# Two transformer blocks and a mixture of experts on one core: GpSimd's subtractions in four pieces, and loop end, latent norm and attention loads in another order

## The chip, the core and the metric

The kernel runs on one core of one Trainium2 chip. A core has TensorE (PE in the rows; PEld is its weight load), VectorE (DVE), ScalarE (ACT), GpSimd (POOL) and a queue for transfers, SyncE (SP). Each engine works through its own list of instructions in the order in which it is written, and waits on semaphores (counters) where it needs another engine's result. The metric is the time of one execution on the device, in microseconds (us); less is better.

## The reference

Two networks run one after the other on 256 tokens of 1024 features, all in float32.

```python
for i in range(2):                       # first network
    sh1, sc1, g1, sh2, sc2, g2 = ada(c, ada_w[i], ada_b[i])     # 6 x 1024 from a 1024 x 6144 matrix
    h_l = rmsnorm(x, norm1_g[i]) * (1 + sc1) + sh1
    if i == 0:   # latent attention over 256 + 256 tokens, beside a short convolution, then w_o
        out_l, _ = even_mixer(h_l, h_c, w_in, ..., w_o)
    else:        # Fourier transform over tokens and features, then w_fourier
        out_l = fourier_mixer(h_l, w_fourier)
    x = x + g1 * out_l
    x = x + g2 * swiglu(rmsnorm(x, norm2_g[i]) * (1 + sc2) + sh2, w1[i], w3[i], w2[i])   # 1024 -> 2816 -> 1024
# second network: window attention and a linear recurrence, then 32 experts, 4 for each token
x = x + gt1 * parallel_mixer(h, ...)
x = x + gt2 * moe_ffn(h, w_router, w_gu, w_down, ...)
return rms_norm(x, g_final)
```

In the latent attention the projection `h @ w_in` has 384 query latents (`cq`), 256 key and value latents (`ckv`) and 32 position features (`k_pe`). The latents are normed, then multiplied by `w_uq` and `w_ukv`.

## The kernel before

Everything lies with features on the 128 partitions and tokens in columns. One launch goes through these stages: the first modulation columns; 18 *blocks* of `w_in`; latent norm, queries and keys; attention in 16 tiles (8 heads by 2 halves of the tokens); 8 blocks of `w_o`; the gated layer of 22 feature slices; the Fourier mixer with 8 blocks; the second gated layer; the second network's mixer; the experts. All of it is written out by hand: the order of instructions on an engine is the order of the code.

**Blocks.** Block `b` is 1024 by 128 weights (512 KB). SP loads it into `raw` (`blk`), once the block three before has been split (`s_hi`, `s_lo`). ScalarE rounds it to the high part `wh` (`block_hi`, L1289), GpSimd subtracts and gets the low part `wl` (`block_lo`, L1711; 34 blocks), and TensorE multiplies in 24 matmuls: high by high, high by low, low by high (`block_product`, L673 to L675). The product of block `b` goes to PSUM bank `b % 2`, so block `b` may start only when VectorE has fetched block `b - 2` (`evacuate`, L1855, which counts `s_ev`). Blocks 10 to 13 (`B_CC`) and 14 to 17 (`B_CU`) belong to the convolution. Blocks 26 to 33 (`B_F`) are those of the Fourier mixer.

**Latent norm.** After block 9 TensorE sums the squares of `cq` and `ckv`, ScalarE takes the roots, and VectorE forms the reciprocals and scales. For `ckv` that stands behind the evacuation of block 10 (`B_CC`): the reciprocal of 512 columns (L1922), two scalings (L1924), one product of `k_pe` (L1926).

**Updates ("ada").** The modulation of later stages is a product of a 1024 by 6144 matrix with one vector. VectorE does it in the gaps: update `n` multiplies a loaded strip of 128x1024 (`araw`, 512 KB) and adds it to `acc` (L1761, or L1760 for the first of eight). `araw` has two buffers: the load of strip `n` is issued when update `n - 2` is done. Every eight updates TensorE turns the sum into columns (`ada_columns`, L609), and the first update of the next eight waits for that. One update stands in each of the first 13 tiles of the attention loop.

**Attention.** For tile `i` TensorE forms scores (L803), VectorE takes the row's maximum (L2008), ScalarE the exponentials (L1401), VectorE the reciprocal of the sum (L2020), ScalarE scales (L1413), TensorE turns the tile (L810) and multiplies by the values (L820).

**Gated layers.** `ffn(l)` runs slices 2 to 21 in loops of four. Its result stands in PSUM, and VectorE adds it to `x` (L2090) after the last product has been counted in `s_fdn`. Then TensorE sums the loop's updates (`loop_rows`, L637), and after ScalarE's squares of `x` (L1299) it forms the norm's sums (`norm_sums`, L654).

## Time and profile before

| What | Value |
|---|---|
| Median of 3 runs | 1834.28 us (1832.84 to 1837.6) |
| The profiled execution | 1836.75 us, its span 1834.5 us |
| TensorE's mean granted clock | 0.958 of full |
| TensorE busy | 1687.9 us (92%) |
| VectorE busy | 778.8 us (42%) |
| ScalarE busy | 421.1 us (23%) |
| GpSimd busy | 103.3 us (6%), 34 subtractions in 92.2 us |
| Read from memory | 584.26 MB, 319 GB/s over the span |

The profiled execution's time is 2.25 us more than its span, and 2.47 us more than the median. Times in the rows count from the start of the span. A row of the timeline gives start, duration, engine, line, operation, what is written and read, how many instructions are merged into the row, and in brackets how long the engine had been idle before it and whose end released it. A row of a table of windows gives each engine's busy time in that stretch, then TensorE's granted clock (1.00 is 2.4 GHz, 0.50 is 1.2 GHz), the share of the transfer engines and their rate.

### The profile page before, as it was taken

The numbers are of one execution on the slowest core, as the hardware profiler recorded it, in microseconds if no ns is written. First come the engines' busy times: TensorE is split into PE (matmuls) and PEld (weight loads), VectorE is DVE, ScalarE is ACT, GpSimd is POOL, SyncE is SP. The second block draws the span as 40 slices with busy tenths as digits, with TensorE's granted clock in tenths as the row PEclk, the third lists the DMA queues.
The fourth block names the chain that finished last, engine by engine and source line by source line (L and its number), as shares of the span: only waits on it lengthen the run. The fifth ranks groups of instructions, "written<-read, shape, count | busy, mean of one in ns | idle before, by whom it ended". The sixth has DMA issues, their size and how long they took to land.

```text
span 1834.5 us, 23890 instructions
## 1 busy us (share of the span) xinstructions
PE 1687.9 (92%) x9312; PEld 1064.2 (58%) x9312; DVE 778.8 (42%) x1230; ACT 421.1 (23%) x669; POOL 103.3 (6%) x53
## 2 busy tenths in 40 slices
PE   6889899999899999999999999999978998799876
PEld 2873489999589999778443434344423443344222
DVE  5757668887548887554221122222201111122012
ACT  2324544443334443363100000000000000000001
POOL 1623010000310000020000000000000000000000
PEclk8898899999999999999999999999988999899988
DMA  8722648887528888615799999999999999999995
GB/s 309 274 81 95 198 133 284 300 309 260 204 81 287 306 310 300 268 68 219 316 407 421 421 421 421 421 421 422 421 421 421 420 422 420 421 414 421 421 421 210
DMA packets 100427, 586.57 MB, mean 320 GB/s; under 512 B 12048, under 2 KB 13328, under 8 KB 44976
## 3 DMA queue, kind: packets, MB, share of 16 engines
q1 hardware_dynamic: 100336, 585.35, 81.4%
q8 instruction: 58, 0.95, 0.2%
q14 instruction: 33, 0.27, 0.0%
HBM read 584.26 MB, written 1.05 MB: 319 GB/s over the span
## 4 chain that ended last, share of the span: by engine, by line
PE 78%; DMA 10%; DVE 6%; SPq 3%; ACT 1%; issue 1%; POOL 0%; DVEq 0%; ACTq 0%
PE psum L1160 23%; PE psum L1176 11%; PE psum L855 4%; PE psum L857 4%; PE psum L856 4%; SPq L418 3%; PE psum L1136 3%; DMA mraw<-gu_dram 3%; PE psum L1189 2%; PE psum L946 2%; PE psum L870 2%; PE psum L869 2%; PE psum L868 2%; DMA araw<-ada_dram 2%; PE psum L1042 2%; PE psum L673 2%
## 5 line engine op out<-in xcount | busy, mean ns | idle before, releaser
L1160 PE MATMUL psum<-mraw,xsat 128*64 128x512 f32 (+2 forms) x1640 | 412.4, 648 | 54.2 <-DMA mraw<-gu_dram 39.6
L1160 PEld LDWEIGHTS psum<-mraw,xsat 128*64 128x64 f32 (+2 forms) x1640 | 136.0, 144 | 305.4 <-issue 304.3
L1176 PE MATMUL psum<-mraw,xsat 128*64 128x512 f32 (+2 forms) x856 | 204.7, 614 | 17.4 <-DMA mraw<-dn_dram 10.2
L855 PE MATMUL psum<-ah,wh 128*128 128x256 f32 x704 | 200.6, 285 | 3.9 <-DVE al L1820 3.6
L856 PE MATMUL psum<-al,wh 128*128 128x256 f32 x704 | 199.2, 283 | 0.0
L857 PE MATMUL psum<-ah,wl 128*128 128x256 f32 x704 | 199.2, 283 | 0.0
L1176 PEld LDWEIGHTS psum<-mraw,xsat 128*64 128x64 f32 (+2 forms) x856 | 68.0, 139 | 133.0 <-issue 130.9
L855 PEld LDWEIGHTS psum<-ah,wh 128*128 128x128 f32 x704 | 135.1, 192 | 6.7 <-DVE al L1820 3.6
L856 PEld LDWEIGHTS psum<-al,wh 128*128 128x128 f32 x704 | 135.1, 192 | 0.0
L857 PEld LDWEIGHTS psum<-ah,wl 128*128 128x128 f32 x704 | 135.1, 192 | 0.0
L2332 DVE TENSOR_TENSOR oacc<-psum,oacc 128x512 f32<-128x512 f32 x60 | 38.7, 686 | 219.9 <-PE psum L1189 219.9
L1160 PE MATMUL psum<-mlast,xsat 128*64 128x512 f32 (+2 forms) x408 | 119.7, 640 | 0.0
L1711 POOL TENSOR_TENSOR wl<-raw,wh 128x1024 fp32r<-128x1024 f32 x34 | 92.2, 2732 | 437.6 <-ACT wh L1289 425.9
L1677 ACT ACTIVATE xsat<-psum 128x512 f32<-128x512 f32 x16 | 9.6, 597 | 432.0 <-PE psum L1209 432.0
L1876 DVE TENSOR_TENSOR wl<-raw,wh 128x1024 fp32r<-128x1024 f32 x88 | 103.7, 1220 | 0.0
L868 PE MATMUL psum<-mh,wh 128*128 128x256 f32 x352 | 99.6, 283 | 0.0
L869 PE MATMUL psum<-ml,wh 128*128 128x256 f32 x352 | 99.6, 283 | 0.0
L870 PE MATMUL psum<-mh,wl 128*128 128x256 f32 x352 | 99.6, 283 | 0.0
L673 PE MATMUL psum<-ah,wh 128*128 128x256 f32 (+1 forms) x272 | 84.0, 309 | 13.8 <-DVE kbuf L1855 6.2
L2344 DVE COPY ymo<-psum 128x512 f32<-128x512 f32 x15 | 10.4, 691 | 196.0 <-PE psum L1176 196.0
L1431 ACT ACTIVATE wh<-raw 128x2048 fp32r<-128x2048 f32 x44 | 83.9, 1907 | 27.4 <-PE psum L675 24.8
L674 PE MATMUL psum<-al,wh 128*128 128x256 f32 (+1 forms) x272 | 82.5, 303 | 0.0
(362 smaller groups left out, 2423.6 us busy)
## 6 DMA issues: line engine op xcount, KB each, us to landing
mraw<-gu_dram SPq DMA_DIRECT2D x205, 1024.0 KB, 19.0
mraw<-dn_dram SPq DMA_DIRECT2D x107, 1024.0 KB, 25.6
araw<-ada_dram SPq DMA_DIRECT2D x128, 512.0 KB, 4.7
mlast<-gu_dram SPq DMA_DIRECT2D x51, 1024.0 KB, 19.7
raw<-ffa_dram SPq DMA_DIRECT2D x44, 1024.0 KB, 7.6
raw<-ffb_dram SPq DMA_DIRECT2D x44, 512.0 KB, 5.7
mlast<-dn_dram SPq DMA_DIRECT2D x21, 1024.0 KB, 23.9
raw<-blk_dram SPq DMA_DIRECT2D x34, 512.0 KB, 4.6
```

Of the source, the lines that this page charges most:

```text
L673: mm(o, wh[:, w], ah3[:, j, 0:width], start=(j == 0), stop=False)
L855: mm(o, wh[:, w0:w0 + P], ah3[:, j, 0:T], start=(j == 0), stop=False)
L856: mm(o, wh[:, w0:w0 + P], al3[:, j, 0:T], start=False, stop=False)
L857: last = mm(o, wl[:, w0:w0 + P], ah3[:, j, 0:T], start=False, stop=(j == DJ - 1))
L868: mm(o, wh[:, w0:w0 + P], a, start=first and j % 2 == 0, stop=False, skip_group_check=True)
L869: mm(o, wh[:, w0:w0 + P], b_, start=False, stop=False, skip_group_check=True)
L870: last = mm(o, wl[:, w0:w0 + P], a, start=False, stop=end, skip_group_check=True)
L1160: last = mm(ps[4 + n][a * w:(a + 1) * w, :], xs[:, k * P + a * w:k * P + (a + 1) * w], slots[slot][:, i * 2 * D + n * 512:i * 2 * D + (n + ...
L1176: last = mm(ps[n][a * w:(a + 1) * w, :], at[:, k * P + a * w:k * P + (a + 1) * w], slots[slot][:, i * D + n * 512:i * D + (n + 1) * 512], ...
L1431: A(wh[:, w], raw[:, w], ACT.Copy).then_inc(s_fhi, 1)
L1711: sub = lambda o, a, b: nc.gpsimd.tensor_tensor(o, a, b.bitcast(F32), ALU.subtract)
L1876: ins = TTn(wl[:, w], raw[:, w], f32(wh[:, w]), ALU.subtract)
```

## The change

It has five parts.

1. `block_lo` does its subtraction in four instructions of 256 columns, not in one of 1024. The semaphore is counted by the last.
2. The norm of `ckv` is spread out: the reciprocal in two halves, and the scalings behind the evacuations of later blocks. TensorE's product that needs the result moves from after block 14 to after block 16.
3. Loads of strips 28 to 34 go between the loads of blocks 24 and 25 and of the first gated slices. Tile 5 of the attention has no update; tile 13 has one.
4. At the end of a gated layer VectorE adds the result to `x` as soon as each pair of feature tiles is finished (a new semaphore, `s_fend`), and two more updates move behind that. ScalarE's rounding of blocks 26 to 28 moves behind the next norm's root, with GpSimd's subtraction of them; blocks 29 to 31 are rounded between copies of the Fourier product.
5. Behind the next norm stand four updates, not two. One semaphore is shared by two uses, so that `s_fend` finds room.

VectorE at the latent norm, blocks 10 to 14 (`rstd` is the reciprocal, `xc` holds `ckv`, `kbuf` the evacuated blocks), before:

```order
L1855 COPY kbuf<-psum 128x256
L1922 RECIPROCAL rstd<-rt 128x512
L1924 SCALAR_TENSOR_TENSOR xc<-xc,vec,rstd 128x512 x2
L1926 TENSOR_SCALAR psq<-kpe,vec 32x512
L1855 COPY kbuf<-psum 128x256 x3
L1911 TENSOR_TENSOR kbuf<-psum,kbuf 128x256 x4
```

and now:

```order
L1866 COPY kbuf<-psum 128x256
L1933 RECIPROCAL rstd<-rt 128x256
L1866 COPY kbuf<-psum 128x256
L1935 RECIPROCAL rstd<-rt 128x256
L1866 COPY kbuf<-psum 128x256
L1938 SCALAR_TENSOR_TENSOR xc<-xc,vec,rstd 128x512
L1866 COPY kbuf<-psum 128x256
L1938 SCALAR_TENSOR_TENSOR xc<-xc,vec,rstd 128x512
L1922 TENSOR_TENSOR kbuf<-psum,kbuf 128x256
L1940 TENSOR_SCALAR psq<-kpe,vec 32x512
```

Each of the three evacuations of blocks 11 to 13 now has at most one longer operation ahead of it.

ScalarE at the end of the first gated layer (`sg`, `mh` are the last slice's; `warm` loads the table for roots; `wh` are the blocks 26 to 31), before:

```order
L1452 ACTIVATE sg<-psum 128x256
L1456 ACTIVATE mh<-mm_ 128x256
L1289 ACTIVATE wh<-raw 128x1024 x3
L1293 ACT_TABLE_LOAD
L1293 ACTIVATE warm<-vec 1x1
L1299 ACTIVATE work<-x 128x256 x8
L1303 ACTIVATE lrow<-psum 128x1024
L1307 ACTIVATE rt<-psum,vec 128x256
L1289 ACTIVATE wh<-raw 128x1024 x3
L1500 ACTIVATE vdft<-psum 128x512 x8
```

and now:

```order
L1465 ACTIVATE sg<-psum 128x256
L1469 ACTIVATE mh<-mm_ 128x256
L1306 ACT_TABLE_LOAD
L1306 ACTIVATE warm<-vec 1x1
L1312 ACTIVATE work<-x 128x256 x8
L1316 ACTIVATE lrow<-psum 128x1024
L1320 ACTIVATE rt<-psum,vec 128x256
L1302 ACTIVATE wh<-raw 128x1024 x3
L1507 ACTIVATE vdft<-psum 128x512 x8
L1510 ACTIVATE ah<-psum 128x256 x2
L1302 ACTIVATE wh<-raw 128x1024
```

The three roundings that stood between the last slice and the squares of `x` stand behind the root.

VectorE at the end of the second gated layer, from the last slice's low part to the mixer's first evacuations (`acc<-araw` are updates 138 to 143, `lam` and `nsink` the second network's small constants), before:

```order
L2053 TENSOR_TENSOR ml<-mm_,mh 128x256
L1761 SCALAR_TENSOR_TENSOR acc<-araw,vec,acc 128x1024 x2
L2090 SCALAR_TENSOR_TENSOR x<-psum,mod,x 128x256 x8
L1761 SCALAR_TENSOR_TENSOR acc<-araw,vec,acc 128x1024 x2
L2114 SCALAR_TENSOR_TENSOR lam<-vec 128x4
L2115 TENSOR_SCALAR hbias<-vec 128x8
L2117 RECIPROCAL rstd<-rt 128x256
L1788 TENSOR_TENSOR mod<-psum,vec 128x40
L1802 SCALAR_TENSOR_TENSOR gs<-mod,vec 128x8
L2121 TENSOR_TENSOR work<-x,rstd 128x256 x8
L1761 SCALAR_TENSOR_TENSOR acc<-araw,vec,acc 128x1024 x2
L2124 TENSOR_SCALAR nsink<-vec 128x8
```

and now:

```order
L2067 TENSOR_TENSOR ml<-mm_,mh 128x256
L2105 SCALAR_TENSOR_TENSOR x<-psum,mod,x 128x256 x8
L1772 SCALAR_TENSOR_TENSOR acc<-araw,vec,acc 128x1024 x2
L2129 SCALAR_TENSOR_TENSOR lam<-vec 128x4
L2130 TENSOR_SCALAR hbias<-vec 128x8
L2132 RECIPROCAL rstd<-rt 128x256
L1799 TENSOR_TENSOR mod<-psum,vec 128x40
L1813 SCALAR_TENSOR_TENSOR gs<-mod,vec 128x8
L2136 TENSOR_TENSOR work<-x,rstd 128x256 x8
L1772 SCALAR_TENSOR_TENSOR acc<-araw,vec,acc 128x1024 x4
L2139 TENSOR_SCALAR nsink<-vec 128x8
```

Two updates moved from ahead of the additions to `x` to behind them, and two from ahead of the reciprocal to behind the norm's products. The diff of the rest:

```diff
@@ SP @@
-            for b in range(B_O + NRAW, B_F):
+            for b in range(B_O + NRAW, B_F - 2):
                 blk(b)
+            ada(28)
+            ada(29)
+            blk(B_F - 2)
+            ada(30)
+            blk(B_F - 1)
+            ada(31)
+            ada(32)
...
                 ffn_a(l, 0, ffna_d[l, 0])
+                if l == 0:
+                    ada(33)
                 ffn_b(l, 0, ffnb_d[l, 0])
                 if l == 0:
+                    ada(34)
                     sp.wait_ge(s_lo, B_O + NRAW)
                 ffn_a(l, 1, ffna_d[l, 1])
@@ PE @@
-                if b == B_CU:
+                if b == B_CU + 2:
                     pe.wait_ge(s_par, MLA_IN)
...
+                        if end and j in (1, 3, 5):
+                            last.then_inc(s_fend, 1)
                     last.then_inc(s_fdn, 1)
@@ POOL @@
             def block_lo(b):
                 pool.wait_ge(s_hi, b + 1)
-                s = slice(SPLIT[b] * D, (SPLIT[b] + 1) * D)
-                sub(wl[:, s], raw[:, RAW[b]:RAW[b] + D], wh[:, s]).then_inc(s_lo, 1)
-
-            for b in range(B_F + NRAW):
+                for q in range(0, D, PIECE):
+                    w0, r0 = SPLIT[b] * D + q, RAW[b] + q
+                    last = sub(wl[:, w0:w0 + PIECE], raw[:, r0:r0 + PIECE], wh[:, w0:w0 + PIECE])
+                last.then_inc(s_lo, 1)
+
+            for b in range(B_F):
                 block_lo(b)
             pool.wait_ge(s_h, 3 * DJ)
-            for b in range(B_F + NRAW, B_2):
+            for b in range(B_F, B_2):
                 block_lo(b)
@@ DVE @@
-                if i < 13:
-                    ada(27 + i)
+                if i < 5 or 6 <= i < 14:
+                    ada(27 + i if i < 5 else 26 + i)
...
-                for j in range(2, 4):
-                    ada(base_n + 40 + j)
-                dve.wait_ge(s_fdn, 1 + (l + 1) * NF)
                 for j in range(DJ):
+                    if j == 6:
+                        dve.wait_ge(s_fdn, 1 + (l + 1) * NF)
+                    elif j % 2 == 0:
+                        dve.wait_ge(s_fend, 3 * l + j // 2 + 1)
                     STT(x[:, j, :], ps[4 + j // 2][:, (j % 2) * T:(j % 2 + 1) * T], m_col(g_gate, j), x[:, j, :],
                         ALU.mult, ALU.add).then_inc(s_x, 1)
-                for j in range(4, 6):
+                for j in range(2, 4):
                     ada(base_n + 40 + j)
```

## Rows read from the trace of the kernel before

**Rows 1.** Table of windows: the experts' stretch; columns as told above
```profile
886.70:1812.00 925.30, 850.25 (x3880) 351.91 (x3876) 176.37 (x324) 50.96 (x81) 0.00 (x0) 0.96 1.01 418
```
**Rows 2.** Whom TensorE waited for before 886 us: total, times, longest
```profile
PE psum L810 <- ACT psq L1413: 10.2, 7, 5.1
...
PE psum L673 <- DVE xc L1855: 4.1, 1, 4.1
```
**Rows 3.** Timeline of VectorE at the latent norm, and TensorE's block 13 behind it
```profile
98.89 3.34 DVE L1922 RECIPROCAL rstd<-rt 128x512 f32<-128x512 f32 x1
102.27 5.13 DVE L1924 SCALAR_TENSOR_TENSOR xc<-xc,vec,rstd 128x512 f32<-128x512 f32 x2
107.44 2.45 DVE L1926 TENSOR_SCALAR psq<-kpe,vec 32x512 f32<-32x512 f32 x1
...
110.49 0.55 PE L673 MATMUL psum<-ah,wh 128*128 128x256 f32 x1 [6.22 <-DVE kbuf L1855]
```
**Rows 4.** Table of windows: TensorE's clock in three stretches at the lower level, one at the upper
```profile
109.24:116.00 6.76, 5.51 (x26) 5.54 (x27) 1.42 (x4) 0.00 (x0) 2.87 (x2) 0.50 0.71 227
...
191.20:198.00 6.80, 4.46 (x12) 2.58 (x13) 5.72 (x12) 4.04 (x8) 0.00 (x0) 0.50 0.57 157
...
215.00:232.00 17.00, 15.32 (x64) 7.78 (x63) 11.51 (x26) 12.44 (x26) 0.00 (x0) 1.00 0.58 174
471.10:477.80 6.70, 3.30 (x8) 2.68 (x9) 0.05 (x1) 6.36 (x13) 4.65 (x2) 0.50 0.98 349
```
**Rows 5.** Timeline of VectorE in the attention: updates 28 and 32
```profile
190.52 1.28 DVE L1761 SCALAR_TENSOR_TENSOR acc<-araw,csil,acc 128x1024 f32<-128x1024 f32 x1 [5.52 <-DMA araw<-ada_dram]
...
206.91 0.75 DVE L1760 TENSOR_SCALAR acc<-araw,csil 128x1024 f32<-128x1024 f32 x1 [5.32 <-PE psum L609]
```
**Rows 6.** Timeline of TensorE: turns of tiles 1, 9 and 11, updates' columns
```profile
186.30 1.06 PE L810 MATMUL psum<-con,psq 128*128 128x128 f32 x4
...
204.86 1.95 PE L609 MATMUL psum<-con,acc 128*128 128x1 f32 x16
...
218.85 0.65 PE L810 MATMUL psum<-con,psq 128*128 128x128 f32 x4 [0.56 <-ACT psq L1413]
...
224.30 0.66 PE L810 MATMUL psum<-con,psq 128*128 128x128 f32 x4 [0.56 <-ACT psq L1413]
```
**Rows 7.** Timeline: one strip's load with the queue empty, and its update
```profile
244.24 0.33 SPq L398 DMA_DIRECT2D araw<-ada_dram  x1
...
248.12 1.28 DVE L1761 SCALAR_TENSOR_TENSOR acc<-araw,csil,acc 128x1024 f32<-128x1024 f32 x1 [1.29 <-DMA araw<-ada_dram]
```
**Rows 8.** Timeline after the gated layers: ScalarE, TensorE (first layer), TensorE (second)
```profile
470.62 2.00 ACT L1289 ACTIVATE wh<-raw 128x1024 fp32r<-128x1024 f32 x2 [9.23 <-DMA raw<-blk_dram]
...
474.50 5.38 PE L654 MATMUL psum<-work,con 128*128 128x256 f32 x16 [6.54 <-ACT work L1299]
...
742.09 3.72 PE L654 MATMUL psum<-work,con 128*128 128x256 f32 x16
```
**Rows 9.** Timeline of VectorE, then TensorE, after the second gated layer
```profile
749.59 2.77 DVE L2121 TENSOR_TENSOR work<-x,rstd 128x256 f32<-128x256 f32 x8
752.28 2.68 DVE L1761 SCALAR_TENSOR_TENSOR acc<-araw,vec,acc 128x1024 f32<-128x1024 f32 x2
...
758.00 0.76 DVE L1855 COPY q<-psum 128x256 f32<-128x256 f32 x2
...
758.57 3.69 PE L946 MATMUL psum<-work,raw 128*128 128x256 f32 x16 [0.27 <-DVE q L1855]
```
**Rows 10.** GpSimd's and VectorE's operations: at the first norm, the context norm, later
```profile
34.00 7.34 POOL L1711 TENSOR_TENSOR wl<-raw,wh 128x1024 fp32r<-128x1024 f32 x3 [33.55 <-ACT wh L1289]
...
54.09 2.58 DVE L1869 TENSOR_TENSOR al<-work,ah 128x256 fp32r<-128x256 f32 x1
...
806.46 0.61 POOL L1735 TENSOR_TENSOR acc<-xg 128x256 f32<-128x256 f32 x1 [57.80 <-ACT xg L1534]
...
818.08 1.32 POOL L1735 TENSOR_TENSOR acc<-xg 128x256 f32<-128x256 f32 x1 [1.20 <-ACT xg L1534]
```

More of the change, by code:

```diff
@@ L47 @@
 NRAW = 3
+PIECE = 256
 SPLIT = [b % 6 for b in range(B_O)] + [0, 1, 4, 5, 2, 3, 4, 5] * 2
@@ L348, in build @@
         s_lg, s_tk, s_tke, s_mask, s_cum, s_route, s_ht, s_htok, s_flag = [sem(n) for n in (
-            "logits", "top_values", "top_exp", "chosen", "slot_counts", "routed", "h_turned", "h_tokens", "overflow_known")]
+            "logits", "top_values", "top_exp", "chosen", "slot_counts", "routed", "tokens_and_output_turned", "h_tokens", "overflow_known")]
         s_order, s_pick, s_gpp, s_gpc = [sem(n) for n in ("experts_ranked", "ranks_set", "places_product", "places_copied")]
@@ L359, in build @@
         s_last = sem("last_output_copied")
-        s_ot, s_fy = sem("out_turned"), sem("final_chunk")
+        s_fy, s_fend = sem("final_chunk"), sem("ffn_last_tiles")
         def sq_cols(n):
@@ L530, in _ @@
             ffn_first(0)
-            for n in range(28, 48):
+            for n in range(35, 48):
                 ada(n)
@@ L1271, in _ @@
                 mm(out_tile(j), ymo[:, j * P:(j + 1) * P], stt[:, (NU - 1) % 3, :], start=False, stop=True,
-                   skip_group_check=True).then_inc(s_ot, 1)
+                   skip_group_check=True).then_inc(s_ht, 1)
             norm_sums(6)
@@ L1477, in ffn @@
                         down_hi(NF - 1, (NF - 1) % 2, 16 * ((NF - 1) // 2 + 1))
-                if l == 0:
-                    act.wait_ge(s_fgu, NF - 1)
-                    block_hi(B_F)
-                    block_hi(B_F + 1)
-                    act.wait_ge(s_fdn, NF)
-                    block_hi(B_F + 2)
             norm_squares(1, x_by_blocks(B_O))
@@ L1495, in _ @@
             act.wait_ge(s_fdn, 1 + NF)
-            for b in range(B_F + NRAW, B_2 - 2):
+            for b in range(B_F, B_F + NRAW):
                 block_hi(b)
@@ L1503, in _ @@
                 A(ah3[:, c, 0:T], ps[c % 2][:, 0:T], ACT.Copy).then_inc(s_f2h, 1)
+                if c in (1, 3, 5):
+                    block_hi(B_F + NRAW + c // 2)
             last_blocks(1, B_2)
@@ L1921, in _ @@
                     dve.wait_ge(s_cqn, 3)
-                    link(V_.reciprocal(rstd[:, :], rt[:, :]))
-                    for j in range(2):
-                        STT(ckv[:, j, :], ckv[:, j, :], V("kvg", j), rstd[:, :], ALU.mult, ALU.mult).then_inc(s_cqn, 1)
+                    link(V_.reciprocal(rstd[:, 0:T], rt[:, 0:T]))
+                if b == B_CC + 1:
+                    link(V_.reciprocal(rstd[:, T:2 * T], rt[:, T:2 * T]))
+                if b in (B_CC + 2, B_CC + 3):
+                    j = b - B_CC - 2
+                    STT(ckv[:, j, :], ckv[:, j, :], V("kvg", j), rstd[:, :], ALU.mult, ALU.mult).then_inc(s_cqn, 1)
+                if b == B_CU:
                     TS(pbuf[NOPE:QD, 0, :], kpe[NOPE:QD, :], vec[NOPE:QD, _V["kgain"]:_V["kgain"] + 1], None, ALU.mult
@@ L2097, in _ @@
             norm(2, _V["n1"] + 8, 6)
-            ada(94)
-            ada(95)
+            for n in range(92, 96):
+                ada(n)
             for c in range(8):
@@ L2121, in _ @@
                 TTn(work[:, j, 0:T], x[:, j, :], rstd[:, 0:T], ALU.mult).then_inc(s_nt, 1)
-            ada(142)
-            ada(143)
+            for n in range(140, 144):
+                ada(n)
             TS(nsink[:, :], vec[:, _V["sink"]:_V["sink"] + 8], -1.0, None, ALU.mult).then_inc(s_ms2, 1)
@@ L2391, in _ @@
             for j in range(DJ):
-                dve.wait_ge(s_ot, j + 1)
+                dve.wait_ge(s_ht, 4 + j + 1)
                 STT(x[:, j, :], out_tile(j), m_col(17, j), x[:, j, :], ALU.mult, ALU.add).then_inc(s_x, 1)
```

## The prediction, made before the changed kernel was run

> **What bounds the kernel now.** I read four views. First the table of windows by stage: from 886.7 us to 1812 us the transfer engines are busy for the whole stretch (share 1.01, 418 GB/s, [rows 1]), and these experts start when TensorE, VectorE and the router before them are done. So a microsecond won or lost ahead of 886.7 us arrives at the end whole, and none of the five parts touches the experts. Second, whom TensorE waited for ahead of that point: ScalarE's scaled tiles, 10.2 us in 7 waits, and VectorE's fetch at the context norm, 4.1 us [rows 2]. Single waits stand as brackets in the timeline, 6.22 us at block 13 behind the latent norm [rows 3]. Third, the granted clock: 0.50 behind each of these stops [rows 4], where the reader is to see the busy time beside the length; at half the rate half of TensorE's busy time is lost. Fourth, the timelines around each stop. In all of this TensorE sets the end, and VectorE or ScalarE sets TensorE's stops.
>
> **Latent norm (part 2).** VectorE does a reciprocal of 3.34, two scalings in 5.13 and a product of 2.45 us in one piece, and TensorE's block 13 waits 6.22 us for the evacuation behind them [rows 3]. Spread out, each evacuation has one piece of 2 to 3 us ahead of it, while a block of TensorE takes about 2.8 us, and the result is wanted two blocks later. So 6.22 us go. The stretch behind it runs at 0.50 with 5.51 us of busy time [rows 4]; without the stop TensorE keeps its upper level, 5.51 / 2 = 2.75 us. Together **-9.0**. What is late next is GpSimd's low part of blocks 16 and 17; from its own operations (their price is below, under the pieces) I work out 109.6 and 112.3 us, and TensorE comes there at 107 and 110 or later: a stop of 0 to 2 us is possible, and I take 0, since its pieces meet fewer two-input operations of VectorE than before.
>
> **Attention loads (part 3).** VectorE waits 5.52 us for strip 28, since its load was issued behind those of the gated slices, and then 5.32 us for the columns of updates 24 to 31 [rows 5]. Undisturbed, tiles 9 and 11 turn 5.45 us apart (218.85, 224.30), so 2.725 us a tile. From tile 1 (186.30) to tile 9 are 32.55 us [rows 6]; eight tiles want 21.8 and the columns 1.95 [rows 6], so 8.8 us are to be had. For the load: strip 28 now leaves when block 24 has been issued, about 180 us, and a strip with an empty queue takes 248.12 - 244.24 = 3.88 us [rows 7]: at 184 us it is there, about 1 us before VectorE comes. Tile 5 without an update takes the columns' wait off. What the new loads are put ahead of are blocks 24 and 25 (wanted at 255 us, no cost) and the first two gated slices; strips 33 and 34 stand between those, and are wanted from tile 7 on. I take 0.5 us off for that, and 0.3 us for a clock that isn't up at once: **-8.0**. Bounds: 9.3 if the last half is free too; 5.1 if TensorE still falls to the lower level as in [rows 4] (191.20 to 198.00, 4.46 us busy), because then the tiles cost about 1.7 us more here and 2 us more in a second such stretch.
>
> **End of the first gated layer (part 4).** ScalarE stands at a rounding of block 27 whose load lands at 470.6 us; behind it wait the squares, and TensorE 6.54 us (467.96 to 474.50) [rows 8]. Now the squares follow the last slice's additions to `x`, made pair by pair while TensorE still multiplies; the last pair is done within 1 us of the product's end, under TensorE's 3.6 us of summing the updates. So 6.54 go. The norm's sums take 5.38 us at 0.50 [rows 4, 8] and 3.72 at 1.00 after the second layer [rows 8]: 1.66 more. Together **-8.2**. Queued behind now: three roundings after the root (2 us for two, [rows 8]), which stand ahead of the Fourier product's copies. TensorE needs 8 us for the norm and the product, so I cost them at nothing. Next in line is the table of the Fourier transform, loaded by 475.2 us, wanted by my count at 476.1: 0.9 us of room, and up to 2 us lost if the load slips.
>
> **End of the second gated layer (parts 4 and 5): a loss.** There is no stop there today: the norm's sums follow the layer at 1.00 [rows 8], since no block's rounding stands in the way. The same code now puts updates 138 to 143 behind. The reciprocal waits for the root; the two updates that filled this now stand behind the norm's eight products, which frees 0.9 us: these end at 751.5 us rather than 752.3 [rows 9]. Then come four updates, not two. Updates 140 and 141 take 2.68 us, the price of the pair now [rows 9]. Strip 142 can be loaded only when update 140 has freed its buffer, at 752.8; with 3.88 us for the load [rows 7] it lands at 756.7, and is used by 758.0; strip 143 follows 1.3 us behind, at 759.4. From the last update to the fetch of `q` VectorE needs 758.00 - (752.28 + 2.68) = 3.04 us of small operations [rows 9], which gives 762.4, so TensorE goes on at 762.9 and not at 758.57 [rows 9]. TensorE's own work ends 0.9 us earlier too: it stands still for some 5.5 us. Net +4.3, and a stop of this size was followed by the lower level in all three places of [rows 4]: +1.7 to +3.4, by the losses of 2.75 and 1.66 above. I take **+7.0**, bounds +3.5 and +9.5.
>
> **Pieces (part 1).** GpSimd's subtraction of 1024 columns takes 7.34 / 3 = 2.45 us, and a VectorE operation with two inputs that meets one takes 2.58 where it needs 0.35 alone (2.77 / 8, [rows 9, 10]). The two take turns by whole instructions. A piece of 256 columns takes 0.61 alone (four: 2.4, so no overhead worth naming) and 1.32 beside VectorE [rows 10]. So the most that one VectorE operation can lose falls from 2.2 to about 0.6 us, but more of them lose it. At the context norm two operations lost 4.3 us together and TensorE 4.1 [rows 2]; now eight stand on the path, 8 x 0.6 = 4.8: +0.5. Elsewhere, at blocks 24 and 25, 0.3 us come back; 34 x 3 more instructions at nothing up to 0.1 us each, off the path. I take **+0.5**, bounds -2 (the operations slip in between pieces at no cost) and +2.
>
> The Trainium skill ("SBUF — State Buffer", section "Who interferes with whom") says that an instruction of VectorE with two inputs in SBUF contends with one of GpSimd that reads there, and that the lock lasts for the whole instruction. By that, smaller pieces would not shorten what is held in all, only deal it out: nothing gained where VectorE has a row of such operations, up to 2 us where it has a single one. The 2.58 us row agrees; that pieces deal it out, no row shows.
>
> **Sum.** -9.0 - 8.0 - 8.2 + 7.0 + 0.5 = -17.7. In the profiled frame 1836.75 - 17.7 = 1819.0; that execution stands 2.47 us above the median, so the median goes from 1834.28 to **1816.5 us**.
>
> **The rivals.**
> First, the clock in the attention stays as it is. For it: four-matmul turns and short products leave TensorE with gaps. Against it: 215 to 232 us runs the same tiles at 1.00 with 15.32 of 17.00 us busy [rows 4]. Then this part gives 5.1: 1819.4 us. With the transform's table late as well, 1821.4; with block 16's low part 2 us late too, 1823.4. The skill ("TensorE: Matmul & The Clock Gate", "Part 4: PE-mode transpose") says that a transpose doesn't count as busy in the same way for the clock, which would keep it down here; the row at 1.00 with the same tiles speaks against that.
> Second, the second layer's stop doesn't come, or the clock holds: strips 140 and 141 lie ready in both versions, so only a faster load of 142 could do it. No stop and no fall: 1809.5. The stop with the clock at 1.00: 1814.
> Third, slower than before: GpSimd becomes what TensorE waits for. For each of the 13 blocks from 5 to 17, between 61.4 and 116.4 us, it has 4.2 us, 1.05 a piece. Above that each microsecond per block costs 13 us, so 17.7 us are gone at 5.6 us a block, 1.4 us a piece. The dearest piece-like row is 1.32, the cheapest 0.61 [rows 10]. Against it: the dear ones stand beside an engine at work throughout. At 1.5 us a piece: 6.0 us a block, 1816.5 + 13 x 1.8 = 1839.9.
> Fourth, the new loads are landed no earlier, since each strip needs its buffer freed by VectorE, and part 3 gives nothing: 1824.5.
>
> **Chances.** The forecast, 1812 to 1821: 0.55. First and fourth rival, 1821 to 1828: 0.2. Second, 1806 to 1812: 0.17. Several stops stay, 1828 to 1840: 0.05. Third: 0.03. The range 1807 to 1827 leaves out 2 in 10. A measurement of this kernel can tell 0.3%, 5.5 us, from no change: faster means below 1828.8, slower above 1839.8. That gives 0.93, 0.04 and 0.03.
>
> **What would show it.** Right: no idle time of TensorE at block 13, clock 1.00 from 104 to 116 us; on VectorE no wait over 1 us for a strip in the attention, and tile 9 some 8 us nearer to tile 1; on ScalarE the squares right behind the last slice and the norm's sums of the first layer in 3.7 us; on VectorE a wait for a strip between updates 141 and 142 of about 2.6 us and on TensorE one of about 5.5 us for `q`, with 0.50 behind it; GpSimd's subtractions x136 at 0.6 to 0.7 us. Wrong: TensorE waiting for `wl` at blocks 16 and 17, for a strip's columns, for the transform's table at 476 us, or more than 5 us at the context norm.

## The result and the profile after

| | Before | Changed |
|---|---|---|
| Median | 1835.22 us (1832.84 to 1837.6) | 1814.7 us (1813.5 to 1819.67) |
| Ratio, 95% interval | | 0.9893 (0.987 to 0.9916) |
| Profiled execution, its span | 1836.75, 1834.5 us | 1813.5, 1811.7 us |
| TensorE busy, mean clock | 1687.9 us, 0.958 | 1679.7 us, 0.961 |
| GpSimd's subtractions | 34 in 92.2 us | 136 in 118.1 us |

Timed once more beside the experiments, the changed kernel gave 1816.75 us and 0.9889 (0.9872 to 0.9905). The gain is 19.6 to 20.4 us by the ratios; 17.7 had been forecast.

To see where it came from I took the same TensorE instruction in both traces and wrote down by how much it starts earlier. Each step between two rows belongs to the stretch between them.

| TensorE instruction | Before | Changed | Difference | Step | Forecast |
|---|---|---|---|---|---|
| first modulation columns, start-up over | 20.53 | 19.22 | -1.31 | -1.3 | 0 |
| block 3, both first norms over | 64.80 | 61.56 | -3.24 | -1.9 | +0.5 (pieces) |
| after block 17 | 125.39 | 113.21 | -12.18 | -8.9 | -9.0 (latent norm) |
| tile 7 of the attention | 214.34 | 193.48 | -20.87 | -8.7 | -8.0 (loads) |
| last of the first layer's norm sums | 477.64 | 448.63 | -29.01 | -8.1 | -8.2 (loop end) |
| Fourier transform begins | 484.52 | 455.84 | -28.68 | +0.3 | 0 |
| the mixer's first block | 750.79 | 720.84 | -29.95 | -1.3 | 0 |
| the same block type, past the stop | 761.02 | 739.32 | -21.70 | +8.2 | |
| last matmul but a few | 1825.46 | 1802.68 | -22.78 | -1.1 | 0 |

The first row is start-up, where only loads are waited for, and no gain: whatever was changed in them, the twelve other traces below stand there 0.8 to 2.0 us earlier than this one of the kernel before. The last two steps around the mixer belong together: -0.9 of the -1.3 is the reciprocal that no longer waits behind two updates, so the second end cost 7.3 us net (forecast +7.0). Now the places one by one.

**Latent norm.** Timeline of VectorE in the changed kernel (start, duration, operation; in brackets the idle time before it), the counterpart of [rows 3]:

```profile
98.22 0.42 DVE L1866 COPY kbuf<-psum 128x256 f32<-128x256 f32 x1 [0.86 <-PE psum L686]
98.56 1.74 DVE L1935 RECIPROCAL rstd<-rt 128x256 f32<-128x256 f32 x1
101.10 0.43 DVE L1866 COPY kbuf<-psum 128x256 f32<-128x256 f32 x1 [0.80 <-PE psum L686]
101.44 0.79 DVE L1938 SCALAR_TENSOR_TENSOR xc<-xc,vec,rstd 128x512 f32<-128x512 f32 x1
103.91 0.42 DVE L1866 COPY kbuf<-psum 128x256 f32<-128x256 f32 x1 [1.68 <-PE psum L686]
104.25 1.22 DVE L1938 SCALAR_TENSOR_TENSOR xc<-xc,vec,rstd 128x512 f32<-128x512 f32 x1
```

Each evacuation now follows TensorE's block (idle before it, released by PE), and the scalings take 0.79 and 1.22 where the pair took 5.13. The window that was at 0.50 in [rows 4] reads, in the changed kernel:

```profile
109.24:116.00 6.76, 6.76 (x56) 6.21 (x54) 0.85 (x2) 0.00 (x0) 1.88 (x3) 1.00 0.78 266
```

TensorE is busy throughout, at 1.00, its upper level. The work has moved by 6 to 12 us within this window, but the clock is 1.00 in all of 92 to 116 us.

**Attention.** VectorE's updates 28 and 32, the counterpart of [rows 5], then TensorE's turns of tiles 1 and 9, of [rows 6]:

```profile
175.32 1.28 DVE L1772 SCALAR_TENSOR_TENSOR acc<-araw,csil,acc 128x1024 f32<-128x1024 f32 x1 [0.38 <-DMA araw<-ada_dram]
...
188.62 0.75 DVE L1771 TENSOR_SCALAR acc<-araw,csil 128x1024 f32<-128x1024 f32 x1 [3.61 <-PE psum L620]
...
173.68 1.06 PE L821 MATMUL psum<-con,psq 128*128 128x128 f32 x4
...
197.63 0.66 PE L821 MATMUL psum<-con,psq 128*128 128x128 f32 x4 [0.56 <-ACT psq L1426]
```

The wait of 5.52 us is 0.38; the one of 5.32 is 3.61 but holds up no tile, since tile 5's work is out of its way. From tile 1 to tile 9 are 23.95 us, 8.6 less than before, and 0.2 more than the 23.75 that the forecast's cadence gives.

**First gated layer's end.** ScalarE, then TensorE, the counterpart of [rows 8], and TensorE's start on the transform:

```profile
439.59 1.28 ACT L1306 ACT_TABLE_LOAD   x1
440.88 0.20 ACT L1306 ACTIVATE warm<-vec 1x1 f32<-1x1 f32 x1
441.94 3.16 ACT L1312 ACTIVATE work<-x 128x256 f32<-128x256 f32 x8 [0.85 <-DVE x L2105]
...
443.46 3.62 PE L648 MATMUL psum<-accl,cone 128*32 128x512 f32 x20
447.02 3.72 PE L665 MATMUL psum<-work,con 128*128 128x256 f32 x16
...
455.84 4.56 PE L913 MATMUL psum<-tabs,work 128*128 128x512 f32 x10 [1.59 <-DMA tabs<-tab_dram]
```

The squares start at 441.94, under the last products; the norm's sums follow without a stop and take 3.72, not 5.38. The transform's table is late by 1.59 us.

**Second gated layer's end.** VectorE, then TensorE, the counterpart of [rows 9]:

```profile
719.64 2.77 DVE L2136 TENSOR_TENSOR work<-x,rstd 128x256 f32<-128x256 f32 x8
722.33 2.68 DVE L1772 SCALAR_TENSOR_TENSOR acc<-araw,vec,acc 128x1024 f32<-128x1024 f32 x2
727.61 1.29 DVE L1772 SCALAR_TENSOR_TENSOR acc<-araw,vec,acc 128x1024 f32<-128x1024 f32 x1 [2.60 <-DMA araw<-ada_dram]
729.71 1.28 DVE L1772 SCALAR_TENSOR_TENSOR acc<-araw,vec,acc 128x1024 f32<-128x1024 f32 x1 [0.81 <-DMA araw<-ada_dram]
730.91 0.17 DVE L2139 TENSOR_SCALAR nsink<-vec 128x8 f32<-128x8 f32 x1
...
734.03 0.75 DVE L1866 COPY q<-psum 128x256 f32<-128x256 f32 x2
...
720.84 7.50 PE L959 MATMUL psum<-work,raw 128*128 128x256 f32 x32 [0.57 <-ACT work L1529]
734.60 7.69 PE L959 MATMUL psum<-work,raw 128*128 128x256 f32 x24 [6.25 <-DVE q L1866]
...
734.60:741.30 6.70, 6.70 (x21) 5.54 (x22) 0.61 (x2) 0.00 (x0) 0.00 (x0) 0.66 0.05 11
```

VectorE waits 2.60 us for strip 142, 0.81 for strip 143, does 3.1 us of small operations, and only then fetches `q`; TensorE stands 6.25 us and goes on at a granted clock of 0.66.

### The profile page after: what moved, and what is told of

The parts are those of the page before. It is cut to its first block, busy times and chain, and to the rows that moved or that the text cites. A ratio compares the mean times of both kernels' runs of the same rounds, so it can differ in the third digit from the quotient of the medians.

```text
span 1811.7 us, 23995 instructions
## 1 busy us (share of the span) xinstructions
PE 1679.7 (93%) x9312; PEld 1058.4 (58%) x9312; DVE 761.2 (42%) x1231; ACT 422.1 (23%) x669; POOL 129.3 (7%) x155
## 4 chain that ended last, share of the span: by engine, by line
PE 80%; DMA 10%; DVE 5%; SPq 3%; ACT 1%; issue 1%; DVEq 0%; ACTq 0%
PE psum L1173 23%; PE psum L1189 10%; PE psum L866 5%; PE psum L867 5%; PE psum L868 5%; SPq L419 3%; PE psum L1149 3%; DMA mraw<-gu_dram 3%; PE psum L1202 3%; PE psum L959 2%; PE psum L881 2%; PE psum L880 2%; PE psum L879 2%; DMA araw<-ada_dram 2%; PE psum L1055 2%; PE psum L684 2%
## 5 line engine op out<-in xcount | busy, mean ns | idle before, releaser
L1720 POOL TENSOR_TENSOR wl<-raw,wh 128x256 fp32r<-128x256 f32 x136 | 118.1, 904 | 384.5 <-DVE work L1857 220.3
```

The source lines that it names most:

```text
L1720: sub = lambda o, a, b: nc.gpsimd.tensor_tensor(o, a, b.bitcast(F32), ALU.subtract)
```

## The experiments

Times are compared with the kernel before, measured beside each of three sets, so the ratios carry the comparison. It took 1837.36 us beside pieces alone, pieces undone and the two runs on the order at the second end; 1836.78 us beside the latent norm alone, the loads alone, ScalarE's order alone and the table's load; 1837.8 us beside halves, eighths, the changed kernel repeated and the old end for both layers. Where I speak of a step, it is read as in the table above, from the profiled execution.

### Part 1: pieces

Pieces alone:

```diff
-                sub(wl[:, s], raw[:, RAW[b]:RAW[b] + D], wh[:, s]).then_inc(s_lo, 1)
+                for q in range(0, D, PIECE):
...
+                    last = sub(wl[:, w0:w0 + PIECE], raw[:, r0:r0 + PIECE], wh[:, w0:w0 + PIECE])
+                last.then_inc(s_lo, 1)
```

> The kernel before with part 1 alone: each of GpSimd's 34 subtractions in four pieces of 256 columns. Theory A (the two traces: TensorE's block 2 starts 1 us earlier against its surroundings, and block 2 to 3 another 1.3): at the context norm TensorE's wait falls by about 2 us; at the latent norm, still in its old form, the two scalings (5.13) and the product (2.45 us) each meet a piece only and take about 2.5 and 0.8 us, so TensorE's 6.22 us wait at block 13 falls to about 2.5. Together 1835.2 - 5.7 = 1829.5 us. Rival B (the forecast: eight operations lose 0.6 each at the context norm): that wait stays at 4.1 or grows, the latent norm gives the same 3.7: 1832. Rival C (the port is held no shorter in all): both waits as before, 1835 us.

Measured: 1834.55 us, ratio 0.9984 (0.9971 to 0.9996): some 3 us, which is B's size. The trace shows A at the latent norm, not at the context norm: TensorE's wait there is 4.00 us, hardly less than 4.11, and block 2 starts 11.40 us after block 0, instead of 11.84. In the latent norm, still in its old order, the pieces shorten the two scalings from 5.13 to 2.31 and the product from 2.45 to 0.83 us, and TensorE's wait at block 13 is 1.77 us, not 6.22:

```profile
98.43 2.31 DVE L1927 SCALAR_TENSOR_TENSOR xc<-xc,vec,rstd 128x512 f32<-128x512 f32 x2
100.78 0.83 DVE L1929 TENSOR_SCALAR psq<-kpe,vec 32x512 f32<-32x512 f32 x1
...
102.21 0.36 PE L674 MATMUL psum<-ah,wh 128*128 128x256 f32 x1 [1.77 <-POOL wl L1712]
```

TensorE is 10.7 us ahead behind block 17. Then it gives back 2.0 at tile 2, where VectorE waits for strip 28 (TensorE's longest wait for a tile is 7.3 us, not 5.1), and 1.5 at the first layer's end, where the load of block 27 took 7.9 us instead of 4.7. Whom TensorE waited for in this run:

```profile
PE psum L811 <- ACT psq L1414: 12.5, 7, 7.3
PE psum L655 <- ACT work L1300: 8.1, 1, 8.1
```

Both stops end with a load, and the load didn't come as much earlier as TensorE did. In this kernel pieces are worth little until these stops are gone.

Pieces undone in the changed kernel (`PIECE = 1024`):

> The changed kernel with part 1 undone (pieces of 1024 columns). Theory A: the context norm's wait is 4.1 us again (+2), and at the latent norm the spread-out scalings take 3 us each, which the time of one block (2.8 us) just hides: 1814.7 + 2.3 = 1817 us. Rival B: nothing at the context norm: 1814.7 us. Rival D (the spread-out norm works only with pieces): a wait of 2 to 3 us at blocks 14 to 17 and the lower clock behind it: 1820 us or more.

Measured: 1821.12 us, ratio 0.9904 (0.9887 to 0.992) against 0.9893 and 0.9889 with pieces: 2 to 3 us, and since the intervals overlap, the size is not settled by the times. The trace bears out A at the latent norm: no stop at blocks 12 to 17 without pieces either (the latent norm's step is -9.0 us), because the scalings of 2.3 us fit inside a block. It does not at the context norm, where TensorE waits 3.44 us, less than with pieces (3.66). D falls. What the pieces bring lies in front of it, and not where I had looked. The eight products behind the first norm, in the kernel without pieces and in the changed one:

```profile
32.29 9.25 DVE L1847 TENSOR_TENSOR work<-xc,rstd 128x256 f32<-128x256 f32 x8
...
32.96 7.62 POOL L1720 TENSOR_TENSOR wl<-raw,wh 128x1024 fp32r<-128x1024 f32 x3 [32.51 <-ACT wh L1302]
```

```profile
32.26 5.97 DVE L1847 TENSOR_TENSOR work<-xc,rstd 128x256 f32<-128x256 f32 x8
...
32.88 9.34 POOL L1720 TENSOR_TENSOR wl<-raw,wh 128x256 fp32r<-128x256 f32 x12 [32.43 <-ACT wh L1302]
```

I had left this row out as off the path. Behind it VectorE takes the modulation columns out of PSUM (L1794), and TensorE's second set of columns waits for that, 1.36 us in the kernel before. In the changed one they wait 1.12 us, and for ScalarE's copy:

```profile
41.39 2.24 PE L639 MATMUL psum<-con,kbuf 64*128 64x2 f32 x16 [1.12 <-ACT kbuf L1342]
```

One pair of traces gives no size here, since TensorE's clock falls at other moments in each. All fourteen do better. This wait is 1.36 to 2.80 us, ended by VectorE, in the six traces with whole subtractions or halves, and 1.12 us, ended by ScalarE, in the eight with quarters or eighths. From the first modulation columns to block 3 TensorE takes 42.9 to 44.8 us in the five traces with whole subtractions (mean 44.1) and 41.5 to 42.9 us in the seven with quarters (mean 42.1). So the pieces bring some 2 us, 0.45 of them at the context norm, and a single trace may be off by more than 1 us.

Halves and eighths (`PIECE = 512`, `PIECE = 128`):

> The changed kernel with GpSimd's subtractions in two pieces of 512 columns. Theory (an operation of VectorE loses the length of one piece each time, and what that costs is decided by where few such operations stand alone): between the forms with one piece and with four. The scaled row of eight behind the first norm took 9.25 us with whole subtractions and 5.97 with quarters; with halves I expect 7.0 to 8.5; the span against the changed kernel +1 to +3 us: 1817 us. Rival: what counts is only that a piece is shorter than an operation of VectorE's pair (0.8 us): halves, 1.2 us, cost as much as whole ones, +4: 1819 us.

> The changed kernel with eight pieces of 128 columns. Theory: VectorE loses 0.25 us a meeting instead of 0.5, the eight products behind the first norm fall from 5.97 to about 4.5 us, but GpSimd itself loses 0.42 us to VectorE at twice as many places and pays a fixed part for each instruction: its 34 subtractions take 130 to 150 us in all, not 118. Blocks whose low part is waited for come later: -1 to +2, 1815 us. Rival: GpSimd becomes what TensorE waits for at blocks 14 to 17 and at strip 28: over +4, 1819 us or more.

Measured: halves 1821.8 us, 0.9915 (0.9889 to 0.9941); eighths 1820.29 us, 0.9909 (0.9892 to 0.9927); beside them the changed kernel:

> The changed kernel itself, once more, so that the others of this set have it beside them. 1814.7 us, and within 3 us of that by what the runs so far scatter; between them TensorE's clock in the stretch from 160 to 168 us decides on up to 2.5 us.

1816.75 us, 0.9889 (0.9872 to 0.9905). By the medians quarters are 3.5 to 5 us better than either, but the intervals overlap. The eight products, with halves and with eighths:

```profile
32.63 9.22 DVE L1847 TENSOR_TENSOR work<-xc,rstd 128x256 f32<-128x256 f32 x8
```

```profile
32.46 4.36 DVE L1847 TENSOR_TENSOR work<-xc,rstd 128x256 f32<-128x256 f32 x8
```

9.25, 9.22, 5.97, 4.36 us: halves bring nothing at all, against what I expected (7.0 to 8.5). Alone the eight take 2.77 us [rows 9], so they lose 6.5, 6.5, 3.2 and 1.6. One product beside GpSimd, with whole subtractions, halves, quarters and eighths:

```profile
35.81 2.57 DVE L1847 TENSOR_TENSOR work<-xc,rstd 128x256 f32<-128x256 f32 x1
...
34.73 1.49 DVE L1847 TENSOR_TENSOR work<-xc,rstd 128x256 f32<-128x256 f32 x1
...
34.68 0.95 DVE L1847 TENSOR_TENSOR work<-xc,rstd 128x256 f32<-128x256 f32 x1
...
34.96 0.67 DVE L1847 TENSOR_TENSOR work<-xc,rstd 128x256 f32<-128x256 f32 x1
```

The losses are a count. GpSimd starts some 0.6 us after the row does (32.88 and 32.26 in the changed kernel), when two or three products are through, so at most six of the eight can meet it. Three whole subtractions meet three products at 2.16 us each; six halves meet six products at 1.08 each; of twelve quarters only six meet a product, 0.53 each; of 24 eighths again six, 0.26 each. A meeting costs 0.2 us less than the piece takes undisturbed (2.35, 1.29, 0.73, 0.45 us). So the loss is about the length of a piece times the smaller of the two numbers, and cutting pays only from where there are more pieces than operations beside them. The number of products was not varied. The Trainium skill ("SBUF — State Buffer", "Who interferes with whom") states an exclusive lock, held for the whole instruction; these rows agree, since a product takes nearly the whole piece on top of its own time.

At the context norm eighths do more than quarters: TensorE's wait there is 1.84 us, where it is 3.66 and 3.99 in the changed kernel's two traces.

Eighths lose on the other side. GpSimd's subtractions take 143.0 us in all (quarters 118.1, halves 103.9, whole 90.8 to 92.2), and TensorE begins to wait for low parts:

```profile
PE psum L684 <- POOL wl L1720: 3.3, 4, 2.0
```

Three of these waits, 1.3 us together, lie between 102 and 110 us. The longest, 2.0 us, is at the last block of `w_o` (243 us); TensorE's clock falls to 0.50 behind it, and with that it loses 3.4 us there, against 0.4 in the changed kernel measured beside it.

### Part 2: the latent norm alone

The diff is part 2 of the change, on the kernel before.

> The kernel before with part 2 alone (the norm of ckv spread over four blocks), GpSimd's subtractions whole. Theory: TensorE's 6.22 us wait at block 13 and the stretch at 0.50 behind it go, 9.0 us, as in the run without pieces: 1837.4 - 9.0 = 1828.4 us. Rival: as in the run with pieces alone, some of it is given back where the next thing waits for a load and not for TensorE (strip 28 in the attention, block 27 at the first gated layer's end): 2 to 4 us of it, so 1831.5 us.

Measured: 1829.38 us, 0.9969 (0.9958 to 0.998): 4 to 8 us. TensorE is 11.2 us ahead behind block 17, with the same step as in the changed kernel (-8.9), and gives 2.4 back at tile 2, where its wait has grown to 7.7 us. VectorE stands for strip 28 there, 7.40 us instead of the 5.52 of [rows 5]:

```profile
181.04 1.28 DVE L1761 SCALAR_TENSOR_TENSOR acc<-araw,csil,acc 128x1024 f32<-128x1024 f32 x1 [7.40 <-DMA araw<-ada_dram]
```

The rival is right about the place in the attention; at the first layer's end nothing was given back in this run.

### Part 3: the attention's loads alone

> The kernel before with part 3 alone (strips 28 to 34 loaded earlier, no update in tile 5). Theory: the waits of VectorE of 5.5 and 5.3 us go, tile 9 comes 8.7 us nearer to tile 1: 1837.4 - 8.5 = 1829 us. Rival: the tiles stay at the lower clock: 1832.5 us. Rival: the wait at the first gated layer's end grows, because it ends with a load: 1831 us.

Measured: 1828.63 us, 0.9963 (0.995 to 0.9977): 4 to 9 us. The steps of the trace between tile 1 and tile 9 are those of the changed kernel (-5.1 at tile 2 and -3.2 more by tile 7, there -4.8 and -3.5), and the lower clock goes from most of the tiles. The wait at the first layer's end is 6.8, not 6.5 us: the second rival had the direction, not the size. Since part 3 takes away the stop at which part 2's gain is lost, the two together should be worth more than one and one; no run has these two alone, so that is argued and not shown. By the ratios the four runs with one part each (pieces, latent norm, loads, ScalarE's order) come to 2.9 + 5.7 + 6.8 + 6.8 = 22.2 us, and all together, with the second end put back (below), to 27.4; the intervals of the five runs are wide enough to hold the difference.

### Part 4: the first end

Only ScalarE's and GpSimd's order of blocks 26 to 31, on the kernel before:

```diff
-                if l == 0:
-                    act.wait_ge(s_fgu, NF - 1)
-                    block_hi(B_F)
-                    block_hi(B_F + 1)
-                    act.wait_ge(s_fdn, NF)
-                    block_hi(B_F + 2)
...
-            for b in range(B_F + NRAW, B_2 - 2):
+            for b in range(B_F, B_F + NRAW):
                 block_hi(b)
```

> The kernel before with only that piece of part 4 which moves ScalarE's roundings of blocks 26 to 31 (and GpSimd's subtractions of them) behind the norm's root. The additions to x stay behind the whole product and behind updates 88 and 89, the second layer's end stays as it was. Theory: this alone takes off TensorE's 6.5 us wait and the lower clock behind it, since the additions to x end at 468.5 us in the kernel before, under TensorE's summing of the updates: 1837.4 - 8.2 = 1829 us, and the semaphore s_fend with the moved updates brings nothing at this end. Rival: the additions are needed earlier too: the wait only falls to 1 to 3 us and the clock still falls: 1833 us.

Measured: 1829.05 us, 0.9963 (0.995 to 0.9977). In the trace TensorE's step here is -8.4 us, all that the changed kernel gets (-8.1):

```profile
463.15 3.23 DVE L2086 SCALAR_TENSOR_TENSOR x<-psum,mod,x 128x256 f32<-128x256 f32 x8 [0.96 <-PE psum L870]
...
463.67 3.16 ACT L1299 ACTIVATE work<-x 128x256 f32<-128x256 f32 x8 [3.01 <-DVE x L2086]
...
463.05 3.62 PE L637 MATMUL psum<-accl,cone 128*32 128x512 f32 x20
466.60 3.72 PE L654 MATMUL psum<-work,con 128*128 128x256 f32 x16
```

The additions start only when the whole product is done (463.15) and end at 466.38, and TensorE goes over from summing the updates to the norm's sums at 466.60 without a stop. The additions pair by pair are not needed. In the kernel before the additions had ended at 468.57, later against TensorE, because one of the two updates ahead of them ran beside GpSimd's subtraction of block 26 and took 3.23 us instead of 1.28. That subtraction has moved too.

### Parts 4 and 5: the second end

The old order of the updates at this end alone, in the changed kernel:

```diff
+                if l == 1:
+                    ada(138)
+                    ada(139)
                 for j in range(DJ):
...
-                for j in range(2, 4):
+                for j in (range(2, 4) if l == 0 else range(4, 6)):
                     ada(base_n + 40 + j)
...
-            for n in range(140, 144):
+            for n in range(142, 144):
                 ada(n)
```

> The changed kernel with the order of the updates at the second gated layer's end as it was before: 138 and 139 ahead of the additions to x, 140 and 141 between these and the reciprocal, 142 and 143 behind the norm's products. Theory: the load of strip 142 waits for update 140, so TensorE's 6.3 us wait for q and the 0.66 clock behind it go away together: 1814.7 - 7.5 = 1807 us, TensorE's wait for q under 0.5 us and no wait of VectorE for a strip over 1 us there. Rival: the additions to x come 2.6 us later by the two updates ahead of them, and TensorE waits for the squares instead, 1 to 2.5 us: 1809 us.

Measured: 1810.14 us, 0.9851 (0.9831 to 0.9871), 6.6 us under the changed kernel's 1816.75 and 4.6 under its 1814.7 (7 or 8 by the ratios). TensorE's waits in the mixer's first blocks:

```profile
PE psum L959 <- ACT work L1529: 1.0, 1, 1.0
PE psum L959 <- DVE q L1866: 0.4, 1, 0.4
```

and its clock there is 1.00 (720 to 740 us). The stop is the order of the updates, and costs some 7 us: 5 to 8 by the times, 7.3 by the trace.

The small operations ahead of updates 142 and 143:

> The changed kernel, but with the chain of small operations (3.1 us) between updates 141 and 142, not behind 143. This parts the stop into its terms. If the strips' loads alone set it, updates 142 and 143 still end at 731 us, q is fetched at 731.0 instead of 734.0, and TensorE waits 3.2 us instead of 6.3; with half of the clock's loss back 1814.7 - 3.5 = 1811 us. If the chain of small operations were the cause, the wait would go altogether: 1807.5 us. If the loads move with the chain, no change: 1814.7 us.

Measured: 1815.13 us, 0.9862 (0.9835 to 0.9888). The stop is halved, from 6.25 to 3.27 us, as the theory has it:

```profile
730.86 1.28 DVE L1772 SCALAR_TENSOR_TENSOR acc<-araw,vec,acc 128x1024 f32<-128x1024 f32 x1
732.64 1.28 DVE L1772 SCALAR_TENSOR_TENSOR acc<-araw,vec,acc 128x1024 f32<-128x1024 f32 x1 [0.50 <-DMA araw<-ada_dram]
733.84 0.74 DVE L1866 COPY q<-psum 128x256 f32<-128x256 f32 x2
...
734.41 9.97 PE L959 MATMUL psum<-work,raw 128*128 128x256 f32 x32 [3.27 <-DVE q L1866]
```

So the two strips and their updates make one half of it, the chain behind them the other. The size isn't settled: the clock fell behind this shorter stop too (0.70 for 9.6 us, 0.76 in the changed kernel), and a second fall some 10 us later, which the changed kernel doesn't have (0.89 for 16 us, there 1.00), took 1.6 us back. That second fall isn't the stop's: the same 1.6 us are lost at this place in five other traces, also in that of the second end put back, where there is no stop. The median lies between the changed kernel's two, the ratio 5 us lower.

Old end on VectorE for both layers, ScalarE's order changed:

```diff
+                for j in range(2, 4):
+                    ada(base_n + 40 + j)
+                dve.wait_ge(s_fdn, 1 + (l + 1) * NF)
                 for j in range(DJ):
-                    if j == 6:
-                        dve.wait_ge(s_fdn, 1 + (l + 1) * NF)
-                    elif j % 2 == 0:
-                        dve.wait_ge(s_fend, 3 * l + j // 2 + 1)
...
```

> The changed kernel with the end of both gated layers on VectorE in its old form: two updates ahead of the additions to x, which wait for the whole product, and two updates, not four, behind the norm. ScalarE's and GpSimd's order stays the changed one. Theory: the additions pair by pair bring nothing at either end, since they lie under TensorE's 3.6 us of summing the updates either way, and the stop for q goes: the same as the run with the second end alone put back, 1810 us. Rival: the additions now end too late for the norm's sums, a wait of TensorE of 1 to 3 us at each end: 1813 to 1815 us.

Measured: 1809.36 us, 0.9853 (0.9837 to 0.987): the same as with only the second end put back, and the lowest median of all. The new semaphore and the split additions bring nothing that can be measured; what part 4 earned, it earned by ScalarE's and GpSimd's order.

The table's load ahead of the strips, with the second end put back:

```diff
                 for b in (B_F, B_F + 2):
                     blk(b)
+                sp.wait_ge(s_pv, HEADS)
+                sp.dma_start(tabs[:, :, :, :], tab_d).then_inc(s_par, 16)
...
```

> The changed kernel with the second gated layer's end back in its old order and, in addition, the load of the Fourier transform's table issued right behind blocks 26 and 28, ahead of six strips and block 27. Theory: the table's wait of 1.6 to 2.1 us goes, nothing else moves: 1810.1 - 2 = 1808 us. Rival: the table's 1 MB delays the strips of updates 86 to 89, VectorE waits for these, the additions to x come late or the root does: 1810 to 1812 us.

Measured: 1810.95 us, 0.9867 (0.9848 to 0.9887): nothing gained over 1810.14. The wait for the table is gone and another stands in its place:

```profile
PE psum L913 <- DVE work L1857: 1.1, 1, 1.1
```

VectorE's modulated columns come 1.1 us after TensorE wants them, as they did in the kernel before. That limit lay right behind the table. With the table late, the step into the transform is +0.3 to +1.25 us in six traces; here it is -0.1. In the changed kernel's second trace the clock fell behind this wait as well, to 0.79 for 8 us, which took 1.7 us more:

```profile
459.17 7.11 PE L913 MATMUL psum<-tabs,work 128*128 128x512 f32 x12 [2.51 <-DMA tabs<-tab_dram]
```

## Why the prediction was right, point by point

- **What bounds the kernel**: right. The differences ahead of the experts (-21.7 at 739 us) arrive at the end (-22.8); in the other traces the experts add or take up to 2 us.
- **Latent norm, -9.0**: measured -8.9, both halves of it (6.4 for the stop, 2.5 for the clock). The 0 for GpSimd's low parts held with whole pieces as well.
- **Attention, -8.0**: measured -8.7. I took 0.8 off the cadence's 8.8 for late strips and the clock. The strips were 0.4 to 1.0 us late for VectorE and mostly hidden. The upper bound of 9.3 didn't follow: the cadence has 8.8 in all.
- **First end, -8.2**: measured -8.1. The step that names ScalarE's roundings as the cause was right. The sentence on the additions pair by pair was right in what it says and silent on the point: with the roundings and subtractions moved, they are hidden without being split. In the kernel before they ended at 468.57 and TensorE's summing at 467.96, and without GpSimd beside it the update ahead of them would have been 1.95 us shorter. I should have asked what part 4 does without them.
- **The table**: 0.9 us of room had been counted, it was late by 1.6. Net cost 0.3 in this trace, since without it VectorE's columns would be 1.1 late; in the changed kernel's second trace it was late by 2.5 and cost 1.25 and another 1.7 by the clock. The term was put at nothing, and its small cost in the first trace is in part luck.
- **Second end, +7.0**: measured +7.3. The stop was 6.25, not 5.5; I had 142 used by 758.0 and the next 1.3 us behind, but strip 143 was used 2.1 us behind strip 142, its load taking 4.6 us with small loads of the mixer beside it. The clock cost 2.3, not 2.7. What I wrote under the rivals, that strips 140 and 141 lie ready in both versions, is wrong for the kernel before, where VectorE waits 2.70 us for strip 140; nothing in the sum rests on it.
- **Pieces, +0.5**: measured -1.9, the one term with the wrong sign. Two steps failed. "Eight on the path, 8 x 0.6": they lost 0.4 to 0.5 each, so the stretch to block 2 became 0.45 us shorter where I had it 0.5 longer. And the row of eight products behind the first norm, which stood in my own reading and took 9.27 us, the prediction doesn't name: I took it to be off the path, by comparing its end with the time of TensorE's next need and not with the operation queued behind it on VectorE. Its part differs from trace to trace: in this pair the columns' wait fell by 0.24 us only, and 1.2 of the 1.9 us are TensorE's clock in blocks 2 and 3, which other traces with whole subtractions don't lose either. That -1.9 lies near the mean of 2.0 over all traces is chance.
- **GpSimd's 0.6 to 0.7 us a piece**: measured 0.90 in the mean, 118 us in all. Two things were missed. The 0.61 us of [rows 10] is another operation, the product of a tile with itself; a piece of the subtraction takes 0.73 undisturbed (37 of 136), against 2.35 for a whole one, so each piece adds some 0.1 us. And 99 of the 136 run beside VectorE, at 0.97. Nothing came of it at this size; at eighths it did.
- **The rivals**: the clock in the attention rose; the second end's stop came; GpSimd never became the bound, at 3.6 us a block with quarters, under the 4.2 that I had worked out; with eighths (4.2 us a block in the mean) TensorE began to wait, 1.3 us in the blocks of that sum and 2.0 at a block outside it. The fourth rival fell: the new loads came earlier (strip 28's update waits 0.38 us).
- **The total**: in the two traces 5.1 us more came than forecast: 2.4 by the pieces, 1.3 by start-up and 1.1 in the experts, which no part touches, 0.7 in the attention, the rest small. By the ratios it is 2 to 3 us more.

## What to carry to other kernels

Where two engines exclude each other by whole instructions, count both sides: the loss is about a piece's length times the smaller number of instructions that can meet, so halving the pieces brings nothing until there are more pieces than operations beside them, and past that the cut engine pays. A gain ahead of a wait that ends with a load can be lost in part at that wait, so look for the next load-bound stop before pricing an edit. And when an order that helps at one place sits in shared code, walk through every other caller: here it gave back 7 us at the second layer, and putting that one back is the better kernel (1809 to 1810 us).

## What the runs showed of the hardware

TensorE's clock is not the same from run to run at the same place. The same eight matmuls ahead of the attention, from two profiled executions of the changed kernel:

```profile
159.77 4.58 PE L774 MATMUL psum<-rt,cone 8*96 8x512 f32 x8
```

```profile
159.25 6.66 PE L774 MATMUL psum<-rt,cone 8*96 8x512 f32 x8
```

Over all the kernels profiled this group of eight took between 4.39 and 7.12 us, the lower level setting in at a different matmul from trace to trace. It isn't the only such place: in the mixer's first stage six of the thirteen others lose 1.6 us against the kernel before, the rest nothing, and it isn't by what was changed in them: the runs with the latent norm alone and with the loads alone are among the six. One place scatters by 2.7 us, more than part 1 is worth, and two traces compared without regard to it would show a gain or a loss that neither kernel has.
